# Interleaving two kinds of matmuls in the up layers of a fused two-block network

## What is computed

```
def squared_relu_mlp(h, w_up, w_down):
    return jnp.square(jax.nn.relu(h @ w_up)) @ w_down

def swiglu(h, w_in, w_out):
    gu = h @ w_in
    gate, up = jnp.split(gu, 2, axis=-1)
    return (jax.nn.silu(gate) * up) @ w_out

x = x + squared_relu_mlp(rms_norm(x, mlp_norm[layer]), w_up[layer], w_down[layer])
x = x + FFN_RES_SCALE * swiglu(rms_norm_2(x, ffn_norm[i, 0]), ffn_w_in[i, 0], ffn_w_out[i, 0])
```

## Time and profile before

| | us |
|---|---|
| median of 3 runs | 1615.61 (1615.54 to 1616.42) |
| the profiled execution | 1616.04 |
| its span in the profile | 1613.1 |
| granted TensorE clock over the span | 0.999 |

### The profile page before, as it was taken

How to read it: one execution, slowest core, us unless ns; L and a number is a source line. 1 busy time by engine, 2 the same in 40 slices (tenths; PEclk the granted TensorE clock), 3 DMA queues, 4 the chain that set the end, 5 groups by cost and what they waited for, 6 DMA issues and landing times.

```text
span 1613.1 us, 25675 instructions
## 1 busy us (share of the span) xinstructions
PE 1599.7 (99%) x9261; PEld 1348.7 (84%) x9261; DVE 1280.8 (79%) x1890; ACT 965.2 (60%) x1466; POOL 89.2 (6%) x117
## 2 busy tenths in 40 slices
PE   9999999999999999999999999999999999999998
PEld 7888888887778888888888888888888888788886
DVE  5987888875969889788884757878878787778887
ACT  7743655555866555666554636565566655866654
POOL 1441000011000000100000000000010000100000
PEclk9999999999999999999999999999999999999999
DMA  9422555573125545555466445554655545245552
GB/s 333 138 100 106 209 182 190 211 287 131 53 81 207 182 182 209 196 199 191 178 245 247 179 157 183 182 191 177 232 183 185 203 185 212 102 154 185 192 193 110
DMA packets 41523, 292.83 MB, mean 182 GB/s; under 512 B 4929, under 2 KB 4961, under 8 KB 7009
## 3 DMA queue, kind: packets, MB, share of 16 engines
q1 hardware_dynamic: 40032, 283.05, 48.2%
q0 software_dynamic: 1264, 8.41, 1.5%
q10 hardware_dynamic: 144, 0.26, 0.0%
HBM read 290.65 MB, written 1.05 MB: 181 GB/s over the span
## 4 chain that ended last, share of the span: by engine, by line
PE 95%; ACT 2%; DVE 2%; issue 1%; POOL 0%; POOLq 0%; DVEq 0%; ACTq 0%
PE ps L787 27%; PE ps L793 14%; PE ps L751 11%; PE ps L753 11%; PE ps L762 11%; PE ps L848 3%; PE ps L849 3%; PE ps L852 3%; PE ps L873 1%; PE ps L1284 1%; PE ps L1079 1%; PE ps L1080 1%; PE ps L1088 1%; PE ps L1606 1%; PE ps L1592 1%
## 5 line engine op out<-in xcount | busy, mean ns | idle before, releaser
L2493 DVE TENSOR_TENSOR w_lo<-raw,w_hi 128x1024 fp32r<-128x1024 f32 x460 | 547.0, 1214 | 103.1 <-ACT w_hi L1778 102.5
L1778 ACT ACTIVATE w_hi<-raw 128x1024 fp32r<-128x1024 f32 x459 | 462.5, 1038 | 132.2 <-PE ps L762 111.8
L787 PE MATMUL ps<-h_both,w_hi 128*128 128x512 f32 x1920 | 461.5, 391 | 0.4 <-DVE h_both L2573 0.2
L787 PEld LDWEIGHTS ps<-h_both,w_hi 128*128 128x128 f32 x1920 | 352.0, 188 | 69.9 <-issue 1.7
L793 PEld LDWEIGHTS ps<-h_both,w_lo 128*128 128x128 f32 x1920 | 247.7, 191 | 10.4
L793 PE MATMUL ps<-h_both,w_lo 128*128 128x256 f32 x1920 | 250.9, 283 | 0.0
L1915 ACT ACTIVATE tm<-ps 128x512 f32<-128x512 f32 x120 | 71.7, 598 | 180.2 <-PE ps L793 179.9
L751 PE MATMUL ps<-w_hi,hid_hi 128*128 128x512 f32 x436 | 170.5, 391 | 0.0
L753 PE MATMUL ps<-w_hi,hid_lo 128*128 128x512 f32 x436 | 169.8, 389 | 0.0
L2650 DVE TENSOR_TENSOR tm<-ps,tm 128x512 f32<-128x512 f32 x120 | 82.9, 691 | 93.5 <-ACT tm L1915 93.1
L751 PE MATMUL ps<-w_hi,h_both 128*128 128x512 f32 x368 | 146.8, 399 | 0.5 <-DVE h_both L2573 0.5
(11 more groups left out here) (429 smaller groups left out, 2002.2 us busy)
## 6 DMA issues: line engine op xcount, KB each, us to landing
raw<-in_stream SPq DMA_DIRECT2D x264, 1024.0 KB, 4.8
ns_w<-in_ns_w POOLq DMA_DIRECT2D x1, 4096.0 KB, 17.7
ln_rows<-in_ln_rows POOLq DMA_DIRECT2D x2, 1024.0 KB, 9.6
row_const<-in_const_rest SPq DMA_DIRECT2D x1, 1076.0 KB, 19.4
raw<-in_second_halves SPq DMA_DIRECT2D x2, 512.0 KB, 7.5
x_sb<-in_x SPq DMA_DIRECT2D x1, 1024.0 KB, 10.0
row_const<-in_fin_rows POOLq DMA_DIRECT2D x2, 512.0 KB, 8.2
out<-x_row SPq DMA_DIRECT2D x3, 256.0 KB, 2.5
```

What stands on the lines that cost most here:

```text
L787: pe.matmul(bank[c], w_hi[:, slot, cols], h_both[:, :, k, :], start=(k == 0), stop=False)
L1778: act.activation(w_hi[:, static % 2, part], raw[:, r % RING, part], ACT.Copy).then_inc(hi_ready, 1)
L2493: dve.tensor_tensor(w_lo[:, static % 2, part], raw[:, r % RING, part], w_hi[:, static % 2, part].bitcast(F32), ALU.subtract).then_inc(lo_r ...
```

## The change

The up layers get a second order of work for all panels but the first two of a layer. In the first half of a panel (k tiles 0 to 3) each high matmul is followed by a low matmul of the panel before (its k tiles 4 to 7); in the second half by one of the panel's own (k tiles 0 to 3). The low product thus runs half a panel behind, and `w_used` is raised in the middle of the following panel. Panel 2 of a layer has 8 high matmuls without a low one, and 8 low ones of the last panel stand alone behind it. Four pairs of banks rotate, `up_bank`: the two of before, then 6 and 7, then 4 and 5. PE waits for the sum of the panel four back; panel 3 of a gated layer waits for `rows_ready`, since bank 4 holds the row of RMS factors until ACT has copied it. ACT's and DVE's programs change only in the bank that they read.

```diff
+        def up_bank(up, bs):
+
+            return (2 * (up.block % 2), 2 * ((up.block + 1) % 2), 6, 4)[bs % 4]
...
+            def low_product(q, b, bs, k, c):
+
+                if k % 4 == 0 and c == 0:
+                    pe.wait_ge(lo_ready, 2 * (q.panel + b) + k // 4 + 1)
+                cols = slice(k * T + c * P, k * T + (c + 1) * P)
+                done = pe.matmul(ps[:, up_bank(q, bs) + c, 0:T], w_lo[:, (q.panel + bs) % 2, cols], h_hi[:, k, :],
+                                 start=False, stop=(k == 7))
+                if k == 7 and c:
+                    done.then_inc(w_used, 1)
+
+            def multiply_lagged(layer, q, b, bs):
+
+                slot, bank = (q.panel + bs) % 2, up_bank(q, bs)
+                if bs == 3 and layer in gated_layers:
+                    pe.wait_ge(rows_ready, gated_layers.index(layer) + 1)
+                if bs >= 4:
+                    pe.wait_ge(hid_sum, hidden_before[layer] + b - 3)
+                for k in range(8):
+                    if k % 4 == 0:
+                        pe.wait_ge(hi_ready, 2 * (q.panel + b) + k // 4 + 1)
+                    for c in range(2):
+                        cols = slice(k * T + c * P, k * T + (c + 1) * P)
+                        pe.matmul(ps[:, bank + c, :], w_hi[:, slot, cols], h_both[:, :, k, :], start=(k == 0), stop=False)
+                        if k >= 4:
+                            low_product(q, b, bs, k - 4, c)
+                        elif bs > 2:
+                            low_product(q, b - 1, bs - 1, k + 4, c)
...
-                first = 2
+                first = 4
...
+                for b in range(2, first):
+                    multiply_lagged(layer, up, b, b)
                 turns, rest = steps(first, up.blocks)
                 with pe.Fori(0, turns) as i:
                     for k in range(RING):
-                        multiply_turned(up, first + RING * i + k, first + k)
+                        multiply_lagged(layer, up, first + RING * i + k, first + k)
                 for b in range(rest, up.blocks):
-                    multiply_turned(up, b, b)
+                    multiply_lagged(layer, up, b, b)
+                for k in range(4, 8):
+                    for c in range(2):
+                        low_product(up, up.blocks - 1, up.blocks - 1, k, c)
...
-                    bank = 2 * ((up.block + bs) % 2)
+                    bank = up_bank(up, bs)
```

## The result

The changed kernel is slower: 1624.53 us median (1622.28 to 1625.27) against 1615.57 (1615.09 to 1616.42), a ratio of 1.0054 [1.0042, 1.0065], or 9.0 us. The forecast was 1614.0, the range ended at 1624.0. The slow rival, put at 1623.5, is what came.

The account below looks back on a forecast made before the run. TensorE, busy 99%, was taken to bound the kernel. Alternating pairs save 2.1 us and waits cost 0.5, so -1.6 us from the 1615.6 median gives 1614.0 us; range 1601.5 to 1624.0.

Parts of the forecast that it names:

- The slow rival: Alternating pairs in up layers: settling never ends, highs cost 232.3 and lows 120 ns; +7.4 us, 1623.5 us; chance 0.22.
- What bounds the kernel: Whole kernel: TensorE busy 99% and never starved in the up layers; only the step of one matmul can change.
- the price of a pair: Alternating high and low in up layers: low 113.3 plus high 233.4, 346.7 ns; 1680 pairs take 582.4 us, 2.1 less.
- 278 is the first low's own: Counter to the slow case: lows settle at once, and only the first low after the highs lasts 278 ns.
- The fast rival: Alternating pairs in up layers: highs stay at 226.7 and lows at 113.3 ns; -13.3 us, 1602.8 us; chance 0.36.
- fits twice over: Counter to the fast case: the high after the lows is slowed although the load it covers fits twice into it.
- Waits: Hand-overs, entries and exits of up layers: shifted waits cost 0.5 us in all, range 0 to 1.0.
- The entry: Start of panel 3 in each ffn layer: PE waits 0.1 us for w_hi, 0.4 us for four layers.
- The steady hand-over to ACT: Each panel's release comes half a panel later, yet conversions stay covered, 1.2 us to spare; missed hand-over: 1624.5 us, chance 0.04.
- The exits of the mlp layers: End of both mlp layers: PE waits between 0 and 0.3 us for the mlp_t conversion, twice.
- Banks at nothing: Bank pairs in up layers: PE waits for the sum four panels back instead of two; nothing waits there before or after.
- The signs to look for: Trace of up layers, low and high durations: 278 and 396 ns forecast, 278 and 389 fast, 283 and 395 slow.

Follow-up runs that it names:

- c2_nudge_inside: Changed kernel with added transposes before the RMS rows (four, two in mlp layers) and two more in the middle of panel 3: 1627.52 us, ratio 1.0086.
- b3_both64: Changed kernel with only 64 of the 128 columns of each alternating high and low product multiplied, so all loads there are half as wide: 1604.85 us.
- b2_low64: Changed kernel with only 64 of the 128 columns of each alternating low product multiplied, highs left full: 1613.61 us against 1615.51 before.
- a1_banks: Kernel before with only the four rotating pairs of banks, highs and lows in the old order: 1615.47 us against 1615.29, ratio 1.0001.
- a2_order: Changed kernel's new order alone, on two pairs of banks, waiting for the sum of the panel two back: 1623.09 us, ratio 1.0050.
- a3_late: Changed kernel alternating from panel 4 on instead of panel 2, with panels 2 and 3 in the old order: 1624.52 us, ratio 1.0057.
- d1_wait_before: Changed kernel with four added transposes behind the RMS rows in ffn layers, so PE reaches panel 3 after the conversion: 1625.10 us, ratio 1.0064.
- b4_nostall: Changed kernel with the special order of ACT and DVE behind a final sum dropped, to convert panel 3 earlier in ffn01, ffn10, ffn11: 1624.43 us, ratio 1.0050.
- d2_both: Changed kernel with three added transposes behind the RMS rows in ffn layers and two among each mlp layer's lone highs: 1619.07 us, ratio 1.0024.

## Why the prediction was wrong

- **What bounds the kernel**: right. PE is busy 99% after as well, nothing starves it, and the loss is in the step of a matmul.
- **The step that failed** is the price of a pair: "what a matmul costs goes by what ran before it", and so the first gain and the first loss cancel at 346.7 ns. The price exists, to the decimal, in ffn10, where the layer is 0.40 us shorter than before; the same price times 1680 was the forecast. Even there it is met by other parts than I had added up: highs of 231.7 and lows of 114.9 ns on average, not 233.4 and 113.3, so that the sum agrees partly by luck. But a matmul's step depends on more than its neighbour: in the slow rhythm a high behind a low takes 233, 241 or 236 ns and a low behind a high 117, 120 or 113. A memory of one step can't give that. The steps can close in two repeating sequences, or three with that of c2_nudge_inside, and the single transitions of the earlier trace rows show none. Between the forecast for the pairs, 582.4 us, and their 592.2 lie 9.8 us: 1336 pairs x 6.7 ns = 8.9, and 0.9 for the stalls.
- **The slow rival** had the idea ("the settling never ends") and nearly the sum: 352.3 ns against a rhythm of 353.3 (the measured mean of 352.5 mixes both rhythms and the stalls). Its parts were off both ways, highs put at 232.3 and measured at 236.3, lows put at 120 and measured at 117.0, so its price is in part luck as well. Its evidence, the 96-column loads that never find their floor within eight matmuls, was the better witness. I gave it 0.22, since its counter ("278 is the first low's own") rested on a low behind *settled* highs, a state that alternation never has. That is the same failing once more: transitions from a settled state were carried over to one that never settles.
- **The fast rival** (340.0) holds in b3_both64, and in b2_low64's ffn10, not with full loads. What I held against it, that the load beside a high "fits twice over", was misread: loads of 128 columns are listed at 187 to 192 ns and a high takes 227, so it fits once.
- **Waits**: sized near, and mispriced. The entry was put at 0.1 us for each ffn layer; it was 0.17, 0.17, 0.3 and none. In ffn01 two errors offset each other: the 8 highs took 1.94 us and not 1.88, which leaves 0.04 of the wait, but 0.14 passed between the conversion's end and the high that waited for it, which the sum had at nothing. In ffn00 the wait isn't all new, since the kernel before has one of 0.22 us at panel 3's start. Its 16 lows ahead of that panel took 2.13 us instead of 1.91:

```profile
665.33 2.07 PE L793 MATMUL ps<-h_both,w_lo 128*128 128x256 f32 x16
667.46 0.49 PE L787 MATMUL ps<-h_both,w_hi 128*128 128x512 f32 x1
```

  But what a stall costs is the rhythm behind it, 2.0 us a layer. "Name the wait and add its length" fails where PE's step remembers. The steady hand-over to ACT held: PE's idle before the highs is 0.2 us in all. The exits of the mlp layers cost a wait of 0.3 us each, the end of the 0 to 0.3, and 0.1 for the slower matmul behind it; those of the ffn layers (0.1 to 0.2 us each) I hadn't priced. The conversion that I had priced was in time; the next one wasn't. ACT, then PE, at the exit of mlp0:

```profile
256.90 1.06 ACT L1836 ACTIVATE w_hi<-mlp_t 128x1024 fp32r<-128x1024 f32 x1 [2.90 <-DVE mlp_t L2545]
258.29 1.06 ACT L1836 ACTIVATE w_hi<-raw 128x1024 fp32r<-128x1024 f32 x1 [0.33 <-DVE raw L2552]
...
258.18 0.40 PE L880 MATMUL ps<-w_hi,mlp_s_hi 128*128 128x512 f32 x1
...
259.40 0.50 PE L880 MATMUL ps<-w_hi,mlp_s_hi 128*128 128x512 f32 x1
```

  258.18 is 2.80 behind the 255.38 of the earlier trace rows, and the layer's start (1.63) and its pairs (1.17) account for that; the product at 259.40 then waits for the second conversion, done at 259.35.
- **Banks at nothing**: right, a1_banks; with two pairs a2_order waited once, in ffn00.
- **The signs to look for**: 283 and 395 for the slow case. The medians are 281 and 398, since each kind has three durations; for the forecast's 278 and 396, ffn10 has 277 and 394; 5.63 us a panel was foretold, 16 x 353.3 = 5.65 came.
- **The range** missed by 0.5 us: the slow case stood at 1623.5, with half a microsecond left for a start of the up layers that alone moves by 1.8 between executions, and for the exits. The changed kernel also spreads over 3.0 us from run to run, the one before over 1.3. A rhythm that falls otherwise in one layer is worth 2; only one execution has a profile, so whether this is the reason stays open.

Open is also why a given sequence of steps falls into the one rhythm or the other, and what the load and the stream share. A run with the entry stall removed and all else equal wasn't achieved; a3_late and d1_wait_before show that slow layers need no stall; the changed kernel, b4_nostall and a2_order show that a stall can make one.

## What to carry to other kernels

A step measured at a transition (the first matmul behind a run of the other kind) isn't the step of a regime made of nothing but transitions: look for a row where the disturbance goes on without end, however far away, and put the heavier chance on what it shows. Narrowing an instruction's operands is a good way to find what disturbs a step (340.0 against 346.7 to 353.3 ns a pair), but no way to win: with 64 columns a matmul makes half the results in the same time. Of the orders tried, the long runs of before were the best that can be relied on. A wait of 0.2 us, or one transpose more or less, can move a loop of 300 pairs by 2%: compare loops layer by layer by their period before taking a difference of some microseconds for the effect of an edit.

## What the hardware showed that I had not expected

- The same loop with the same instructions has two lasting periods, 693 ns for two pairs and 1060 ns for three, and in two layers a third, 347 ns for each pair, and holds any of them for over 100 us. The steps of the last highs ahead of the loop went with which one came in all 54 starts; a stall can change it, and once it changed where a load began 10 ns behind its matmul instead of 2 to 5.
- With one high and one low in turn, the price of a pair comes in steps of 6.7 ns: 340.0, 346.7, 353.3. Narrowing only the low matmuls, whose loads run beside the highs, takes one step off either rhythm (346.7 and 340.0); narrowing both leaves 340.0 alone.
- A high's step depends on the load that runs beside it although its 227 ns cover that load: with 128 columns the load is listed at 188 ns and the highs of mlp0 take 237 on average, with 64 columns it is listed at 138 ns and they take 229 (b2_low64). Whether it is the load or the narrower low matmul, no run separates.
- Waiting can pay: d2_both, with three transposes that have no use ahead of each ffn layer, is faster than the kernel it was made from, though not than the kernel before.
